# Modulation columns as row products on VectorE in place of weight-streaming matmuls: a two-block transformer on one core

## The reference, cut to what matters

```python
c_act = silu(c)                                   # [1, 1024]
for l in range(2):                                # first block
    mod = c_act @ ada_w[l] + ada_b[l]             # 6 x 1024 values: sh1, sc1, g1, sh2, sc2, g2
    xm = rms_norm(x) * (1 + sc1) + sh1
    x = x + g1 * ((gates * attention, pooling of xm @ w_in[l]) @ w_out[l])
    xf = rms_norm(x) * (1 + sc2) + sh2
    x = x + g2 * peer_ffn(xf)                     # 16384 experts, 16 chosen per head and token
s_c, s_cc = silu(c_2), silu(c_ctx_2)              # second block: latent and context vector
for i in range(2):
    m  = s_c  @ ada_w_2[i] + ada_b_2[i]           # 9 x 1024 values, for x
    mc = s_cc @ ada_w_2[i] + ada_b_2[i]           # the same matrix, for the context (only 5 x 1024 of layer 0 are used)
    x = half_step_ffn(x); x = mixer(x, ctx); x = half_step_ffn(x)
```

## Time and profile before

| | |
|---|---|
| time, median of 3 runs | 3757.21 us (3756.78 to 3763.63) |
| the profiled execution's own time | 3760.27 us |
| its span | 3758.1 us |
| TensorE busy (matmul) | 3591.4 us, 96% |
| VectorE busy | 2690.9 us, 72% |
| ScalarE busy | 2034.6 us, 54% |
| POOL busy | 217.2 us, 6% |
| mean granted TensorE clock | 0.985 |
| row products (L1119) | 152, 1225 ns each |
| ada matmul records (L2072) | 704 in 88 units |
| moved by DMA | 784.65 MB, mean 209 GB/s |

### The profile page before, as it was taken

The page is one execution under the profiler, slowest core; times in us unless marked ns, Lnnn a source line. Parts: engine busy times, 40 slices in busy tenths (PEclk is TensorE's granted clock), DMA queues, the critical chain, the costliest instruction groups (busy, mean ns, idle before and its releaser), DMA issues.

```text
span 3758.1 us, 71030 instructions
## 1 busy us (share of the span) xinstructions
PE 3591.4 (96%) x24950; PEld 3281.8 (87%) x24950; DVE 2690.9 (72%) x5336; ACT 2034.6 (54%) x4235; POOL 217.2 (6%) x335
## 2 busy tenths in 40 slices
PE   5989999999999989999999998999998899999898
PEld 5889999998888889999998887899987689898898
DVE  6774986667777664896667777777777577776765
ACT  4544447775555554447775555544444454545444
POOL 0000111110000000111110001010001010100000
PEclk8999999999999999999999999999999999999999
DMA  8456776667775434776647778776765167575453
GB/s 281 154 187 213 269 269 213 213 220 240 242 241 190 137 129 168 249 264 230 214 170 254 242 240 252 229 246 214 245 219 168 32 201 248 197 247 167 140 185 133
DMA packets 245507, 784.65 MB, mean 209 GB/s; under 512 B 30048, under 2 KB 62816, under 8 KB 245040
## 3 DMA queue, kind: packets, MB, share of 16 engines
q1 hardware_dynamic: 230544, 737.78, 59.5%
q0 software_dynamic: 14752, 44.12, 3.3%
HBM read 747.17 MB, written 34.60 MB: 208 GB/s over the span
## 4 chain that ended last, share of the span: by engine, by line
PE 77%; DVE 7%; PEld 6%; issue 3%; DMA 3%; ACT 2%; PEldq 1%; SPq 0%; ACTq 0%; POOL 0%; DVEq 0%
PE bank L1906 17%; PE bank L1907 17%; PE bank L1908 17%; PE bank L1979 5%; PE bank L1980 5%; PE bank L1981 5%; PE bank L2200 3%; PEld bank L1979 2%; PEld bank L1980 2%; PEld bank L1981 2%; DVE wl L1101 2%; DMA raw<-stream 2%; PE bank L2050 2%; PE bank L2072 1%; ACT wh L643 1%
## 5 line engine op out<-in xcount | busy, mean ns | idle before, releaser
L1101 DVE TENSOR_TENSOR wl<-raw,wh 128x512 fp32r<-128x512 f32 x2180 | 1453.8, 690 | 687.2 <-ACT wh L643 684.8
L643 ACT ACTIVATE wh<-raw 128x512 fp32r<-128x512 f32 x2180 | 1316.5, 629 | 825.3 <-PE bank L1981 427.0
L1906 PE MATMUL bank<-XH,wh 128*128 128x256 f32 x5184 | 1504.0, 290 | 88.0 <-DVE XL L1226 49.9
L1907 PE MATMUL bank<-XL,wh 128*128 128x256 f32 x5184 | 1477.4, 285 | 0.0
L1908 PE MATMUL bank<-XH,wl 128*128 128x256 f32 x5184 | 1476.6, 285 | 0.0
L1906 PEld LDWEIGHTS bank<-XH,wh 128*128 128x128 f32 x5184 | 1004.4, 194 | 129.6 <-issue 92.0
L1907 PEld LDWEIGHTS bank<-XL,wh 128*128 128x128 f32 x5184 | 1005.9, 194 | 4.0 <-issue 1.0
L1908 PEld LDWEIGHTS bank<-XH,wl 128*128 128x128 f32 x5184 | 1004.7, 194 | 0.0
L1979 PE MATMUL bank<-wh,AH 128*128 128x512 f32 x1464 | 571.4, 390 | 1.4 <-DVE AL L1609 1.0
L1980 PE MATMUL bank<-wl,AH 128*128 128x512 f32 x1464 | 570.8, 390 | 0.0
L1981 PE MATMUL bank<-wh,AL 128*128 128x512 f32 x1464 | 569.6, 389 | 0.0
(11 more groups left out here) (237 smaller groups left out, 3146.4 us busy)
## 6 DMA issues: line engine op xcount, KB each, us to landing
raw<-stream SPq DMA_DIRECT2D x1340, 512.0 KB, 4.3
h_spill<-side POOLq DMA_DIRECT2D x256, 128.0 KB, 3.7
side<-h_spill SPq DMA_DIRECT2D x256, 128.0 KB, 3.8
arena<-rpb POOLq DMA_DIRECT2D x4, 1024.0 KB, 25.3
arena<-tables POOLq DMA_DIRECT2D x2, 832.0 KB, 9.5
X<-x_t POOLq DMA_DIRECT2D x1, 1024.0 KB, 8.2
side<-ctx_t POOLq DMA_DIRECT2D x8, 128.0 KB, 3.9
arena<-ctx_t POOLq DMA_DIRECT2D x1, 1024.0 KB, 8.3
```

The costliest lines, as they stand in the source:

```text
L643: act.activation(wh[:, n % 4, :], raw[:, q % 4, HALF * half:HALF * (half + 1)], ACT.Copy).then_inc(hi_ready, 1)
L1101: tt_op(wl[:, n % 4, :], raw[:, q % 4, HALF * half:HALF * (half + 1)], wh[:, n % 4, :].bitcast(F32), SUB).then_inc(lo_ready, 1)
L1906: pe.matmul(out, wh[:, n % 4, a:b], moving_h, start=start, stop=False, skip_group_check=check)
L1907: pe.matmul(out, wh[:, n % 4, a:b], moving_l, start=False, stop=False, skip_group_check=check)
```

## The change

All modulation columns become folds. The 88 ada units, the tile `vectors`, the block copies and turns go. `fold1` is split in two names of 48 (one per layer), `fold2` covers all 144 columns of the second block. New places: 16 folds after units 66, 69, ... 111 of expert_u.0 (layer 1's first 16 columns); 32 folds beside w_in.1, attn_o.1, w_out.1, query.1 at the units of layer 0; 8 `fold2` folds after units 0, 4, ... 28 of query.1; 16 after units 66, 69, ... 111 of expert_u.1; 19, 21, 10 beside ffn.0.0, ffn.0.0.x, kv_ctx as before; 14 beside qkv (units 0 and 2 are new); 21 and 21 beside ffn.0.1 and ffn.1.0 as before; 6 beside conv_in and 8 beside ffn.1.1 (both had none). The first 40 `fold2` columns (16 in expert_u.1, 19 in ffn.0.0, 5 in ffn.0.0.x) are needed for the context vector too: there a second row product with the context's silu is issued ahead of the first, from the same unit. The silu of c stays in `c_kept`; c_2 and c_ctx are loaded at the start by POOL ahead of x (2 x 512 KB), silu is taken once, and both are stored in a DRAM scratch `c_spill` (2 x 512 KB), from which POOL reloads them for query.1, expert_u.1, ffn.0.0 and over `c_kept` (4 x 512 KB in all, one of them in place of the load of c_2). In layer 1 the tables' DMA stands behind two of these reloads, which wait for the operand of w_in.1. The choices' feed points become more: 65 units are fed before the gates instead of 60, and the 64 batches are laid over the units 65 to 124, so that four units carry two. Biases are added in smaller pieces, each behind its folds. The order lists grow: conv_in, ffn.1.1 and layer 1's products are written out instead of looped on VectorE, ScalarE and SP where the code asks for `mixed_stages`.

```diff
-MIXED_ADA = ("ada1.1", "ada2.0")
-MIXED_U = (120, 100)
-TURN_AT, GATES_FROM = 57, 60
-EXP_AT = (26, 53)
+TURN_AT, GATES_FROM = 62, 65
+EXP_AT = (30, 59)
...
+    def beside_layer(l, name, columns):
+        put(f"w_in.{l}", (2, 3, 4, 6, 7, 8, 10, 11, 12, 14, 16, 18, 20, 22, 24, 26), name, columns[0:16])
+        put(f"attn_o.{l}", (1, 3, 5, 7), name, columns[16:20])
+        put(f"w_out.{l}", (1, 2, 4, 5), name, columns[20:24])
+        put(f"query.{l}", range(2, 32, 4), name, columns[24:32])
...
+    beside_layer(0, "fold1.0", one[16:48])
+    put("expert_u.0", range(66, 114, 3), "fold1.1", one[0:16])
+    beside_layer(1, "fold1.1", one[16:48])
+    two = list(range(DEPTH * 72))
+    put("query.1", range(0, 32, 4), "fold2", two[40:48])
+    put("expert_u.1", range(66, 114, 3), "fold2", two[0:16])
+    put("ffn.0.0", rows_of(range(2, 21)), "fold2", two[16:35])
+    put("ffn.0.0.x", rows_of(range(21)), "fold2", two[35:40] + two[48:64])
...
+    put("qkv", (0, 1, 2, 3, 5, 7, 9, 11, 13, 15, 17, 19, 21, 23), "fold2", two[74:88])
...
+    put("conv_in", range(1, 13, 2), "fold2", two[130:136])
+    put("ffn.1.1", rows_of(range(8)), "fold2", two[136:144])
...
+    def batches_of(u):
+        return [b for b in range(BATCHES) if GATES_FROM + 15 * b // 16 == u]
...
     def _(pool):
+        for n in range(2):
+            pool.dma_start(c_rows_at[:, n * D:(n + 1) * D], c_rows[1 + n, :, :]).then_inc(rows_loaded, 16)
         pool.dma_start(X[:, :, :], x_in).then_inc(x_loaded, 16)
...
             if l:
+                pool.wait_ge(xl_ready, made["w_in.1"])
+                pool.dma_start(c_query, c_spill[0, :, :].rearrange("p (n w) -> p n w", w=D // 2))\
+                    .then_inc(query_c_loaded, 16)
+                pool.dma_start(c_experts, c_spill[0, :, :].rearrange("p (n w) -> p n w", w=D // 2))\
+                    .then_inc(experts_c_loaded, 16)
                 pool.wait_ge(space_free, l)
             pool.dma_start(A(TAB1, 2 * T + P + POOL_GROUPS * T),
                            tables[:, at1:at1 + 2 * T + P + POOL_GROUPS * T]).then_inc(tables_loaded, 16)
+            if l == 0:
+                pool.wait_ge(c_ready, 2)
+                for n in range(2):
+                    pool.dma_start(c_spill[n, :, :], c_rows_at[:, n * D:(n + 1) * D]).then_inc(c_stored, 16)
+                pool.wait_ge(c_stored, 32)
...
             unit = raw[:, q % 4, :].rearrange("p (n w) -> p n w", w=D // 2)
+            if name == "fold2" and n < 40:
+                dve.wait_ge(context_c_loaded, 16)
+                dve.scalar_tensor_tensor(unread, unit, 1.0, c_kept[:, :, :], MUL, MUL,
+                                         accum_out=second_mod(0, n, n + 1, 1))
             dve.scalar_tensor_tensor(unit, unit, 1.0, c, MUL, MUL, accum_out=dst).then_inc(folded, 1)
...
                 for n in range(LISTS):
                     step(nc.vector.max(vals[:, n, 0:8], scores[:, n, :]))
-                    if n % 8 == 7:
+                    if n % 5 == 4:
                         feed()
...
                 for n in range(LISTS):
                     step(nc.vector.max_index(idxu[:, n, 8:16], vals[:, n, 8:16], repl[:, n, :]))
-                    if n % 8 == 7:
+                    if n % 4 == 3:
                         feed()
...
             for b in range(BATCHES):
-                feed()
+                while fed[0] <= GATES_FROM + 15 * b // 16:
+                    feed()
...
         def context_inverse():
             invert(rms)
+            add_bias(0, 2, 24, 40, sides=2)
             operand_coefficients(0, 24, 1, "ln_g.0.0", "ln_b.0.0")
...
             for u in range(KEYS):
                 pe.wait_ge(group_free, U.g + u + 1)
                 tile(U, u, 0, 0, banks[4 + (U.g + u) % 2][:, 0:T], first_pair)
-                for a in after(l, u):
-                    ada_unit(first_block + a // KT, a % KT, place[MIXED_ADA[l], a])
-                n = block_after(l, u, 3)
-                if n is not None:
-                    turn_block(first_block + n)
...
-                b = u - GATES_FROM - 1
-                if 0 <= b < BATCHES:
+                for b in batches_of(u - 1):
                     spread_choices(b)
```

More of the change, by code:

```diff
@@ L152, in plan @@
     fold_at = {}
-    for name, units in (("fold1", 48), ("fold2", FOLDED_2)):
+    for name, units in (("fold1.0", 48), ("fold1.1", 48), ("fold2", 72 * DEPTH)):
         fold_at[name] = placed
         placed += units
-    order = [("fold1", k) for k in range(FIRST_FOLDS)]
+    order = [("fold1.0", k) for k in range(FIRST_FOLDS)]
     starts = {}
     for name, units, split, source, groups in rows:
-        if name in MIXED_ADA:
-            continue
         starts[name] = len(order)
@@ L250, in __call__, with build @@
         return self.at[name]
-def build(nc, ctx, stream, columns, tables, x_in, ctx_in, rpb, c_rows, h_spill, out):
+def build(nc, ctx, stream, columns, tables, x_in, ctx_in, rpb, c_rows, h_spill, c_spill, out):
     stages, order, place, spans, folded_units, fold_at, _ = plan()
@@ L460, in build, with folds_by @@
     block = ctx.enter_context(nc.Block())
-    BLOCKS = [stages[name].units // KT for name in MIXED_ADA]
-    def after(l, u):
-        return [2 * (u // 5) + u % 5 // 2] if u < MIXED_U[l] and u % 5 in (0, 2) else []
+    def folds_by(name, k):
+        return folded_units.index((name, k)) + 1
+    def batches_of(u):
+        return [b for b in range(BATCHES) if GATES_FROM + 15 * b // 16 == u]
     CTX_FROM = 103
@@ L474, in ctx_tile_at @@
         return k if rest == 0 and 0 <= k < KT else None
-    def block_after(l, u, late):
-        n, rest = divmod(u - late - 17, 20)
-        return n if rest == 0 and 0 <= n < BLOCKS[l] else None
     mixed_stages = {name for name, _ in fold_after}
@@ L899, in row_highs @@
                 act.activation(AH[:, j % 2, :], AP_[:, j % 2, :], ACT.Copy).then_inc(row_high, 1)
-            first, first_block = l * BATCHES, BLOCKS[0] * l
-            used = stages[MIXED_ADA[l]].r
+            first = l * BATCHES
             for u in range(KEYS):
@@ L1256, in scale_plus_one, with add_bias @@
                 settle()
-        def add_bias(l, which, a, b, sides=1, placed=0, units=0):
-            if placed:
-                dve.wait_ge(block_placed, placed)
-            if units:
-                dve.wait_ge(folded, units)
+        def add_bias(l, which, a, b, sides=1):
+            last = (f"fold1.{l}", b - 1) if which == 1 else ("fold2", 72 * l + b - 1)
+            dve.wait_ge(folded, folds_by(*last))
             if which == 1:
@@ L1266, in add_bias @@
             else:
-                bias = column(f"ada_b_2.{l}", a, b - a)
-                view = mod2[:, l, a:b, 0:sides]
-                step(tt_op(view, view, bias.unsqueeze(2).broadcast_to([P, b - a, sides]), ADD))
+                for side in range(sides):
+                    view = second_mod(l, a, b, side)
+                    step(tt_op(view, view, column(f"ada_b_2.{l}", a, b - a), ADD))
             settle()
@@ L1317, in _ @@
                 for n in range(FIRST_FOLDS):
-                    fold("fold1", n)
+                    fold("start", "fold1.0", n)
                 dve.wait_ge(prepared, 48)
-                add_bias(0, 1, 0, 16, units=FIRST_FOLDS)
+                add_bias(0, 1, 0, 16)
                 scale_plus_one(scale[:, :], mod1[:, l, 8:16], column(f"norm_mix.{l}", 0, KT))
@@ L2054, in mean_square @@
             column_mean(tiles(sq, KT), bank, squares_ready, "squares_ready")
-        def turn_block(n):
-            pe.wait_ge(block_copied, n + 1)
-            if n >= 2:
-                pe.wait_ge(block_placed, n - 1)
-            for f in range(2):
-                last = pe.transpose(banks[2 + n % 2][:, f * P:(f + 1) * P],
-                                    rows[:, (n % 2) * BLOCK + f * P:(n % 2) * BLOCK + (f + 1) * P], ident[:, :])
-            last.then_inc(block_turned, 1)
-        def ada_unit(n, kt, q):
-            if kt == 0 and n >= 2:
-                pe.wait_ge(block_copied, n - 1)
-            pe.wait_ge(raw_ready[q % 4], 16 * (q // 4 + 1))
-            for g in range(GROUPS):
-                matmul = pe.matmul(banks[6 + n % 2][GROUP * g:GROUP * (g + 1), 0:BLOCK], vectors[:, kt, :],
-                                   raw[:, q % 4, BLOCK * g:BLOCK * (g + 1)], start=kt == 0, stop=kt == KT - 1,
-                                   tile_position=(0, GROUP * g))
-            matmul.then_inc(raw_used, 1)
         pe.wait_ge(prepared, 48)
-        pe.wait_ge(constants_set, 5)
+        pe.wait_ge(constants_set, 4)
         for l in range(DEPTH):
```

204 lines of the change are left out of this document (78 added, 126 removed).

## The result

The changed kernel takes **3773.22 us** (median of 7 runs, 3769.51 to 3777.75), the kernel before on the same chip 3762.6 (7 runs, 3756.78 to 3764.41): ratio 1.0033, 95% interval 1.0021 to 1.0044. It is slightly slower, where 3726 and "faster" were forecast. The profiled execution took 3777.75 us, its span is 3775.9. It is the slowest of the seven: the two profiled executions lie 17.5 us apart (3777.75 and 3760.27), the medians 10.6.

The account below looks back on a forecast made before the run. TensorE was taken to run without a gap in the expert stages. Gross gain 75 less 12 (choices) and 10 (batches) gives 53; added costs 5.5, 5, 6, 1.7, 2.4, 0.4 leave -32 us: 3726 us, range 3700 to 3748.

Parts of the forecast that it names:

- Four units with two batches: Expert batches: spreads in doubled units wait for ScalarE's bank copy, 5 us per layer, bounds 0 and 9.
- Removal: Expert stages: 88 ada units at 0.75 us and 11 block turns leave TensorE's path; gross gain 75 us with waits.
- Choices: Expert choices with 65 units: VectorE's second part of each half lags TensorE, 6 us of waiting per layer, bounds 0 and 11.
- Folds in the batches at 0: Expert batches: folds fit into VectorE's waits for spreads, cost 0 to 3 us, taken as 0.
- Price of a row product: VectorE: 1225 ns each from the trace, used instead of 2.45 us by the skill's halved-throughput rule.
- Start: Kernel start: POOL's extra loads and stores compete with a nearly full DMA stream, +5 us, bounds 2 and 7.
- Layer 1 to sub_keys: w_in to query in layer 1: 32 folds, eight more in query.1, reloads and tables, +5.5 us, bounds 2 and 10.
- ffn.0.0: 19 folds become double; the added product goes straight through in groups with an operand piece, +6 us, bounds 2 and 12.
- Later stages: ffn.0.0.x +1.7 us for a doubled fold and biases, qkv +2.4 us for two more folds.
- (a): Rival, all hidden: no stalls in expert_u, gain 75 us, other stages cost 13, 3695 us; chance 0.13.
- (b): Rival, VectorE sets the pace: stalls in choices, batches and ffn.0.0 at their upper bounds, 3749 us; chance 0.17.
- (c): Rival, slower: 128 added row products, 157 us of VectorE, all on the path, 3839 us; chance 0.08.

Follow-up runs that it names:

- before_doubled: Kernel before, all its ada units kept, with only the batches placed so that four units carry two, feeds to match: 3795.90 us, ratio to before 1.0098.
- ring_open: Changed kernel, doubled units kept, VectorE's low halves ahead of certain one-hots and ScalarE's bank copies ahead of gelu, those weightings behind it: 3727.87 us, ratio to before 0.9924.
- copies_first: Changed kernel with only ScalarE's order moved around doubled units: bank copies ahead of gelu, certain weightings behind it: 3743.89 us, ratio to before 0.9961.
- single61: Changed kernel with 61 units fed before the gates and one batch per unit, choices' feeds thinned by four a layer: 3723.70 us, ratio to before 0.9904.
- single61_late: single61 with four POOL DMAs moved later, two stores and two reloads of c: 3718.13 us, ratio to before 0.9886.
- single61_noctx: single61 without the 24 context row products in ffn.0.0 and ffn.0.0.x, so that part is not computed: 3715.66 us, ratio to before 0.9881.
- columns: single61_late with four two-product columns moved into layer 1's batches; ffn.0.0 groups 5, 7, 8, 9 get one-product folds: 3710.74 us, ratio to before 0.9869.

## Why the prediction was wrong

**The step that failed** is "Four units with two batches": 5 us per layer, bounds 0 and 9. The runs show 22 and 25 us in the changed kernel, and 37 us in two layers with nothing else changed (before_doubled). The step had the right kind of wait, a spread ahead of ScalarE's copy, and the profile after shows it at L2154. It was followed through one link alone, from the earlier trace rows: copy ready at 643.90 against a spread at 642.83, a delay of 1.07. Two things were missed. First, the same two-deep rule also holds VectorE's second one-hot and ScalarE's weighting, and those have low halves, gelu and copies queued behind them; the step never asked what stands behind a waiting instruction on its engine. Second, a delayed copy delays the next unit's handshake again, so the effect lasts three units. Even the upper bound, "twice that per doubling", multiplied the wrong base.

**The rest of the sum stands.** In ring_open, where only that stall is taken away, the experts of layer 0 are 30.9 us shorter and of layer 1 23.3, against 29.6 (37.2 + 3.4 - 6 - 5) and 23 in the forecast, and the whole is 3727.9 against 3726. That both agree is in part luck: ring_open has no batch stalls where I had 5 a layer, and more waiting in the choices. Point by point:
- *Removal*: right. An ada unit was paid in full; 0.75 us each came off wherever no new wait took it.
- *Choices*: 9 us a layer for 6, within its bounds; the periods of 3.40 are as forecast, the 3.36 and 4.22 ahead of them are not.
- *Folds in the batches at 0*: right. Every third unit keeps 3.77, in layer 1 with two products.
- *Price of a row product*: 1218 to 1225 ns in the four groups of after, 1225 in the earlier trace rows. The halved throughput that the Trainium skill states (Vector Engine (DVE) Microarchitecture Reference, section 7) adds nothing on top of the listed time: in the rows of ffn.0.0 above the second product starts 1.23 us behind the first (2418.61, 2419.84).
- *Start*: +4.9 for +5. *Layer 1 to sub_keys*: +8.2 for 5.5, within 2 to 10; the DMA wait of 7.26 is there, and the forecast had named it.
- *ffn.0.0*: +7.3 and the 1.14 us of group 5's added product ahead of the inverse, for +6. 1.4 of the 7.3 is a lower clock that the sum did not have (last section); without it, in copies_first, the stretch is +5.8. *Later stages*: +3.1 for +4.1.

**The rivals.** (a), all hidden, fell on both conditions: the copies came late, and the choices wait 9 us a layer. Its price was added up wrongly as well: it puts the other stages at 13 us where the sum has 21, so it should have been 3703. (b) came nearest in kind, all stall terms at their upper bounds, but its price for the batches (18) was under half of what they cost (47). (c), products on the path, is refuted: single61 has all 128 of them and is 1% faster. "Slower by 0.2%" came true by a mechanism that the prediction listed only as a small term. The chances were too sure because the one new coupling between engines was priced from one pair of rows.

## What to carry to other kernels

Doubling one stage's work per step in a software pipeline is not a local edit: with buffers n deep, step b+1 waits for step b+1-n, and if that one sits behind the same step's long instruction, everything queued behind each wait on each in-order engine moves too. Write for each engine what stands behind the wait, and go round until nothing is late; here the two engines' orders gave some 0 and 27 us alone and 41 together (by the ratios). Compare such a doubling with the version that does without it: 61 units and one batch each had the whole gain.

## What the runs showed of the hardware

TensorE's stalls can cost more than their length, where the clock falls behind them. The granted clock (PEclk, the third column from the right) in the kernel after around the doubled unit:

```profile
641.00:643.00 2.00, 1.76 (x10) 1.76 (x11) 0.75 (x2) 1.32 (x4) 0.54 (x1) 0.71 0.38 84
643.00:645.00 2.00, 2.00 (x12) 2.00 (x11) 2.00 (x4) 1.18 (x4) 0.00 (x0) 0.50 0.64 244
```

Behind the waits of 1.48 and 2.18 us it is 0.50 of full speed, the lower level of 1.2 GHz, and the tile that starts at 642.46 has its matmuls 0.21 us apart where 0.12 is usual. The doubled unit 110 shows the price: its waits are the same (1.48, 2.18, 0.96), but its clock stays at 1.00, and its three periods add up to 17.57 us against 19.10 of unit 80. That is 1.5 us, about a fifth of the 6.9 that unit 80 costs. In ring_open the clock of that whole stretch is 1.00.

The same happens at the start of ffn.0.0. Behind the inverse TensorE waits 1.80 us for the low halves in the kernel after (0.66 before) and 1.81 in copies_first, which differs only in the experts. The ten us from each inverse on, kernel after and copies_first:

```profile
2410.00:2420.00 10.00, 8.20 (x52) 7.70 (x52) 8.12 (x15) 2.41 (x5) 0.00 (x0) 0.83 0.56 163
```

```profile
2380.30:2390.30 10.00, 8.19 (x60) 7.43 (x59) 9.54 (x16) 2.48 (x6) 0.00 (x0) 1.00 0.65 203
```

The clock falls in the one and not in the other, and ffn.0.0 takes 206.09 and 204.66 us. (single61 and single61_late have the lower clock there too, the kernel before, single61_noctx and columns have not.) So equal waits were followed by either clock; what decides is not shown here. The forecast priced a short stall of the bounding engine at its length; in these places it cost 1.4 to 1.5 us more.
